# Last stage of a hybrid attention and expert-routed layer on one core: early unscaled residual rows, a ninth weight piece ahead, and single depth steps in the first expert pair

## The chip, the cores and the metric

The kernel runs on one core of a Trainium2 chip. The metric is device time in microseconds (us) of one execution; the kernel before took 2093.07 us (median of three runs, 2092.68 to 2094.48).

## The reference, cut to what matters

One layer for 512 latent tokens of width 2048 (and 256 context tokens, which only give keys and values). All is fp32. Only the second half bears on the change:

```python
x = x + mod_lat[:, 2] * merge_heads(o_m, o_n, g_out_mla[l], g_out_na[l], w_out[l])
h2 = modulate(rms_norm(x, g_norm2[l]), mod_lat[:, 3], mod_lat[:, 4])
x = x + mod_lat[:, 5] * expert_choice_ffn(h2, w_router[l], w_gate[l], w_up[l], w_down[l])

def expert_choice_ffn(h, w_router, w_gate, w_up, w_down):
    aff = softmax(h @ w_router)                  # 16 experts
    g, idx = top_k(aff.T, cap)                   # each expert picks cap = 64 tokens
    xs = h[idx]
    y = (silu(xs @ w_gate) * (xs @ w_up)) @ w_down * g[..., None]
    return zeros.at[idx].add(y)
```

## The kernel before, in words

The first 880 us compute the modulation, the projections and the attention. What follows is staged like this.

**Output projection.** `OUT_PLAN` orders four column blocks of 512, each in two halves of the depth (so eight steps `p`), each over four tiles of 128 tokens. DVE adds every result to the residual `x1` in SBUF (`residual`, L1837 and L1842; semaphore `x1_add`). SyncE (SP) loads the projection's weights, 2 MB a step (`load_w_out`, L605). In the last step, each finished tile is turned (`turn_x1`, L973), multiplied with the router's weights (`route`, L985), its softmax taken on DVE and ACT (`soft`), and the result turned again (`turn_aff`, L1006).

**The choice.** DVE finds each expert's 64 best tokens in eight rounds (L1911, L1913) and marks them (L1915). TensorE turns the marks (L1029) and counts them with a triangular and a ones matrix (L1035); DVE makes the slot numbers (L1921) and from them `member` (L1931), the 0/1 matrix that picks the 128 rows of an expert pair. ACT meanwhile scales `x1` in place by the reciprocal root of each row's mean square (L1408, `x1_scaled`), four tiles.

**The experts.** There are 8 pairs of experts. The weights of one pair are 24 pieces of 2 MB: 16 of gate and up (one for each depth step of 128, `gate_up`, L1115) and 8 of down (`down`, L1145). All 192 pieces are loaded by SP in order (`moe_load`, L657). Eight (`PRE`) go to slots of their own before any is used. After that a piece goes into one of six slots (`RING`), and its load waits until the piece that had the slot is used: the semaphore `moe_used` counts the pieces that TensorE has finished. `SLOT_AT` says where the slots lie; slots 6 and 7 are used once and then hold the accumulators.

```python
for n in range(PRE, PAIRS * PIECES):
    before = n - PRE if n < PRE + RING else n - RING
    sp.wait_ge(moe_used, before + 1)
    moe_load(n)
```

The rows of a pair are picked by products of `x1` with `member`, four depth steps at a time (`gather`, L1064), and taken, scaled and shifted by DVE (`take_xsT`, L1953). In pair 0 these groups stand before the depth steps 0, 2, 6 and 10. Pair 1's rows come another way: the scaled `x1` is stored to HBM as `x1_d` (L673, by SP, behind the eight first pieces and the load of `gate2_b`, L668), `find_rows` (L1072) gives the numbers of the rows, and GpSimd fetches them with an indirect DMA (L1560). `turn_member` (L1088) and `rows_of` (L1081) are two short groups of products at depth steps 12 and 13; the weights that `rows_of` gives are taken by DVE in `take_rows`. After the 16th piece ACT takes the silu (L1424), DVE multiplies (L2008), TensorE turns the result (L1131), and the down pieces follow. `spread` (L1102, L1103) adds the rows back.

The queues that matter here: SP issues every weight load and, before, the stores of `x1_d`; each of its waits holds everything behind it. ACT issues none in this stage, and GpSimd the one gather.

## Time and profile before

| | |
|---|---|
| median of 3 runs | 2093.07 us |
| profiled execution | 2088.43 us |
| its span on the core | 2086.5 us |
| TensorE matmuls busy | 1938.2 us (93%) |
| weight loads of TensorE | 1231.2 us (59%) |
| DVE / ACT / GpSimd busy | 832.6 / 427.1 / 174.4 us |
| moved by DMA | 602.78 MB, mean 289 GB/s |
| mean granted TensorE clock | 0.987 |

The page cuts the span into 40 slices of 52.2 us. Slice 21 (from 1095 us) is where the experts' weights begin. All rows below give times in us from the start of the span.

### The profile page before, as it was taken

Reading aid. Unit: us, or ns where it says so; the run is one execution under the profiler, and the core shown is the slowest. Engines: PE = TensorE matmul, PEld = TensorE weight load, DVE = VectorE, ACT = ScalarE, POOL = GpSimd, SP = SyncE. Lnnn points to the kernel's source line nnn. Section 1 sums busy time; section 2 is a strip of 40 time slices with the busy share of each in tenths; the row PEclk is TensorE's granted clock in tenths of the full one; section 3 lists DMA queues with packets and bytes.
Section 4 is the critical chain, followed back from the end, with each engine's and each line's share of the span. In section 5 each row is a group of like instructions: output and inputs, shape, how many; then the busy total and the mean of one; then the engine's idle time right before and its main releaser. Section 6 shows DMA issues by size and latency. Waiting matters only on the chain.

```text
span 2086.5 us, 25707 instructions
## 1 busy us (share of the span) xinstructions
PE 1938.2 (93%) x10114; PEld 1231.2 (59%) x10114; DVE 832.6 (40%) x1723; ACT 427.1 (20%) x1141; POOL 174.4 (8%) x402
## 2 busy tenths in 40 slices
PE   4899999999999999989996999998989999898988
PEld 2578788878877777768885533433435353443433
DVE  5557877773245555534444131221303021121303
ACT  4223223122145555532222000000000000000000
POOL 0003112011133322200000000000000000000000
PEclk9999999999999999999997999999999999999999
DMA  9937888783122111132228999999999999999998
GB/s 403 421 141 270 325 294 291 270 282 138 46 102 86 45 44 44 43 134 81 81 81 353 395 419 429 427 427 428 427 428 427 428 427 427 428 428 427 426 428 355
DMA packets 77079, 602.78 MB, mean 289 GB/s; under 512 B 7568, under 2 KB 25232, under 8 KB 33568
## 3 DMA queue, kind: packets, MB, share of 16 engines
q1 hardware_dynamic: 64224, 591.11, 70.0%
q10 hardware_dynamic: 12592, 8.98, 1.3%
q8 instruction: 81, 1.33, 0.3%
q0 software_dynamic: 144, 1.05, 0.1%
q14 instruction: 38, 0.31, 0.0%
HBM read 584.32 MB, written 16.79 MB: 288 GB/s over the span
## 4 chain that ended last, share of the span: by engine, by line
PE 50%; DMA 11%; DVE 2%; ACT 2%; issue 1%; POOL 0%; DVEq 0%; ACTq 0%
DMA arena<-in_w_gate_up 10%; PE SM L1115 7%; PE TM L1115 7%; PE SM L1145 6%; PE TM L1145 5%; PE TR L1064 3%; PE MJ L1064 2%; PE TM L919 1%; PE SM L885 1%; PE SN L1102 1%; DMA wor<-in_w_out 1%; PE MJ L817 1%; PE MJ L821 1%; PE SM L890 1%; PE SM L960 1%
## 5 line engine op out<-in xcount | busy, mean ns | idle before, releaser
L1115 PE MATMUL SM<-arena 128*64 128x512 f32 x1024 | 245.0, 598 | 47.2 <-DMA arena<-in_w_gate_up 46.7
L1115 PE MATMUL TM<-arena 128*64 128x512 f32 x1024 | 242.7, 592 | 0.0
L1683 DVE SCALAR_TENSOR_TENSOR arena<-arena,csil 128x512 f32<-128x512 f32 x240 | 180.3, 751 | 46.7 <-DMA arena<-in_w_mod 38.3
L1115 PEld LDWEIGHTS SM<-arena 128*64 128x64 f32 x1024 | 71.0, 136 | 191.4 <-issue 190.5
L1115 PEld LDWEIGHTS TM<-arena 128*64 128x64 f32 x1024 | 78.6, 137 | 141.1 <-issue 141.1
L1145 PE MATMUL SM<-arena 128*64 128x512 f32 x512 | 117.8, 609 | 1.5 <-DVE arena L2011 1.5
L1145 PE MATMUL TM<-arena 128*64 128x512 f32 x512 | 116.9, 599 | 0.0
L1203 ACT ACTIVATE wh<-wr 128x2048 fp32r<-128x2048 f32 (+1 forms) x32 | 58.7, 1835 | 192.4 <-PE TN L720 148.8
L1931 DVE TENSOR_TENSOR arena<-cst,rope_t 128x512 f32<-128x512 f32 x8 | 5.5, 692 | 230.3 <-PE MJ L1088 230.3
L718 PE MATMUL SM<-wh,h_hi 128*128 128x512 f32 (+1 forms) x224 | 89.2, 398 | 7.8 <-DVE h_lo L1631 7.8
L1413 ACT CAST y_hi<-arena 128x512 fp32r<-128x512 f32 x32 | 19.8, 619 | 367.7 <-DVE arena L1967 367.7
L1419 ACT CAST memberT<-MJ 128x512 fp32r<-128x512 f32 x8 | 4.7, 585 | 435.7 <-PE MJ L1088 435.7
L1989 DVE TENSOR_TENSOR arena<-arena,SN 128x512 f32<-128x512 f32 x56 | 38.3, 684 | 123.0 <-PE SN L1103 123.0
L718 PE MATMUL TM<-wh,h_hi 128*128 128x512 f32 (+1 forms) x224 | 87.3, 390 | 0.0
L720 PE MATMUL SM<-wh,h_lo 128*128 128x512 f32 (+1 forms) x224 | 85.9, 384 | 0.0
L719 PE MATMUL SM<-wl,h_hi 128*128 128x512 f32 (+1 forms) x224 | 85.7, 383 | 0.0
L1440 POOL TENSOR_TENSOR st<-st,halves 128x1 f32<-128x1 f32 (+2 forms) x116 | 81.9, 706 | 41.7 <-DVE st L1598 32.1
L720 PE MATMUL TM<-wh,h_lo 128*128 128x512 f32 (+1 forms) x224 | 85.1, 380 | 0.0
L719 PE MATMUL TM<-wl,h_hi 128*128 128x512 f32 (+1 forms) x224 | 85.0, 379 | 0.0
L1609 DVE TENSOR_TENSOR wl<-wr,wh 128x2048 fp32r<-128x2048 f32 (+1 forms) x32 | 70.0, 2186 | 26.8 <-ACT wh L1203 26.7
L1145 PEld LDWEIGHTS SM<-arena 128*64 128x64 f32 x512 | 35.3, 139 | 68.7 <-issue 65.3
L1145 PEld LDWEIGHTS TM<-arena 128*64 128x64 f32 x512 | 33.9, 136 | 66.5 <-issue 66.5
(327 smaller groups left out, 3488.1 us busy)
## 6 DMA issues: line engine op xcount, KB each, us to landing
arena<-in_w_gate_up SPq DMA_DIRECT2D x128, 2048.0 KB, 16.3
arena<-in_w_down SPq DMA_DIRECT2D x64, 2048.0 KB, 25.5
arena<-in_w_mod SPq DMA_DIRECT2D x96, 1024.0 KB, 5.5
wr<-in_w_na SPq DMA_DIRECT2D x24, 1024.0 KB, 7.0
wor<-in_w_out SPq DMA_DIRECT2D x8, 2048.0 KB, 7.9
xT<-in_tokens_t SPq DMA_DIRECT2D x4, 1536.0 KB, 12.6
arena<-in_w_qkv SPq DMA_DIRECT2D x8, 640.0 KB, 5.4
wr<-in_w_qa SPq DMA_DIRECT2D x4, 1024.0 KB, 11.9
```

What stands on the lines that cost most here:

```text
L718: pe.matmul(dst, h_hi[:, k, rows], w_hi[w % 2][:, cols], start=first, stop=False)
L719: pe.matmul(dst, h_hi[:, k, rows], w_lo[w % 3][:, cols], start=False, stop=False)
L720: return pe.matmul(dst, h_lo[:, k, rows], w_hi[w % 2][:, cols], start=False, stop=last)
L817: mm = pe.matmul(MJ[:, 0:QK], cqT[:, k, i * P:(i + 1) * P], wq[g % 2][:, k, :], start=(k == 0), stop=(k == Q_RANK // P - 1))
L1064: mm = pe.matmul(dst[:, i * P:(i + 1) * P], x1[:, tile, k * P:(k + 1) * P], member[:, tile, :], start=(tile == 0), stop=(tile == LT - 1))
L1115: mm = pe.matmul(GU[b][64 * e:64 * e + CAP, :], xsT[:, k, 64 * e:64 * e + CAP], w[:, 2 * (b // 2) + e, (b % 2) * NB:(b % 2 + 1) * NB], sta ...
L1145: mm = pe.matmul(GU[b][64 * e:64 * e + CAP, :], actT[:, f, 64 * e:64 * e + CAP], w[:, 2 * j + e, :], start=(f == 0), stop=(f == KF - 1))
L1203: sc.activation(w_hi[w % 2][:, 0:n], w_raw[w % 3][:, 0:n], ACT.Copy).then_inc(w_high, 1)
L1440: po.tensor_tensor(out_ap, ms, halves[:, 0:n], ALU.pow).then_inc(done, 1)
L1609: ve.tensor_tensor(w_lo[w % 3][:, 0:n], w_raw[w % 3][:, 0:n], w_hi[w % 2][:, 0:n].bitcast(F32), ALU.subtract).then_inc(w_low, 1)
L1683: ve.scalar_tensor_tensor(acc, row, c, acc, ALU.mult, ALU.add).then_inc(mod_step, 1)
L1989: ve.tensor_tensor(dst, dst, src, ALU.add).then_inc(acc_done, 1)
```

## The change

- `x1_d` is stored without scaling and by column blocks: the first three blocks by SP behind the weights of the projection's steps 3, 5 and 7, the last by ACT, tile by tile, after each tile's `route`. ACT's scaling of `x1` in place now waits for all 16 of these stores. The fetched rows of pair 1 are scaled afterwards by ACT; their factors come out of `find_rows` beside the row numbers (`rows_rs`).
- `PRE` is 9: the ninth piece goes to a new slot 8, where `gate1_b`, `gated` and `x1T` were and `gate2_b`, `act` and `actT` will be. It waits for the last residual and the last `route`. `gate2_b` is loaded later, ahead of load number 15, after the tenth piece is used. `member_1` moves to other space.
- Pieces 4 to 7 wait for the last projection result (`y_full`) and no more for DVE's reading of it (`y_free`).
- In pair 0 the rows are picked one depth step at a time (`gather_first`, `take_first`): steps 0 and 1 ahead of piece 0, then step k + 2 behind piece k. `turn_member` and `rows_of` move to behind the depth steps 14 and 15.
- TensorE runs 77 products of constants (`keep_clock`), in six places from the end of the projection to the first pick.

The diff, cut to its core:

```diff
-PRE = 8
+PRE = 9
-SLOT_AT = [4, 5, 0, 2, 6, 7, 1, 3]
+SLOT_AT = [4, 5, 0, 2, 6, 7, 1, 3, 8]
@@ sync
                 load_w_out(p)
+                if p >= 3 and p % 2:
+                    nb = p // 2 - 1
+                    cols = slice(nb * NB, (nb + 1) * NB)
+                    sp.wait_ge(x1_add, LT * (2 * nb + 2))
+                    for tile in range(LT):
+                        sp.dma_start(x1_d[tile * P:(tile + 1) * P, cols], x1[:, tile, cols]).then_inc(x1_out, 16)
             sp.wait_ge(y_full, LT * (2 * MODB - 1))
             for n in range(4):
                 moe_load(n)
-            sp.wait_ge(y_free, LT * 2 * MODB)
-            for n in range(4, PRE):
+            sp.wait_ge(y_full, LT * 2 * MODB)
+            for n in range(4, PRE - 1):
                 moe_load(n)
-            sp.dma_start(gate2_b[:], modrow_d[1:2, :].partition_broadcast(P)).then_inc(gate2_in, 16)
-            for tile in range(LT):
-                sp.wait_ge(x1_scaled, tile + 1)
-                sp.dma_start(x1_d[tile * P:(tile + 1) * P, :], x1[:, tile, :]).then_inc(x1_out, 16)
+            sp.wait_ge(x1_add, LT * 2 * MODB)
+            sp.wait_ge(lg_part, LT * MODB)
+            moe_load(PRE - 1)
             for n in range(PRE, PAIRS * PIECES):
                 before = n - PRE if n < PRE + RING else n - RING
                 sp.wait_ge(moe_used, before + 1)
+                if before == PRE:
+                    sp.dma_start(gate2_b[:], modrow_d[1:2, :].partition_broadcast(P)).then_inc(gate2_in, 16)
                 moe_load(n)
@@ tensor
+            def keep_clock(n):
+                for i in range(n):
+                    pe.matmul(SM[:, 0:P], ident[:], ones[:], start=True, stop=True)
...
                 elif kind == "x1_turn":
+                    if (a, tile) == (MODB - 1, LT - 1):
+                        pe.wait_ge(y_free, LT * 2 * MODB - 1)
+                        keep_clock(7)
                     turn_x1(a, tile)
                 elif kind == "route":
+                    if (a, tile) == (MODB - 1, LT - 1):
+                        keep_clock(2)
                     route(a, tile)
...
+            keep_clock(7)
             turn_aff(LT - 1)
+            keep_clock(56)
...
+            def gather_first(k):
+                if k == 0:
+                    pe.wait_ge(member_set, 1)
+                    pe.wait_ge(x1_scaled, LT)
+                if k >= 2:
+                    pe.wait_ge(xt2_free, k - 1)
+                for tile in range(LT):
+                    mm = pe.matmul((TR, MJ)[k % 2][:, 0:P], x1[:, tile, k * P:(k + 1) * P], member[:, tile, :],
+                                   start=(tile == 0), stop=(tile == LT - 1))
+                mm.then_inc(xt2_full, 1)
...
                 for k in range(KD):
-                    if pair == 0 and k in (0, 2, 6, 10):
-                        gather(0, (k + 2) // 4)
-                        if k == 2:
-                            find_rows()
+                    if pair == 0 and k == 0:
+                        gather_first(0)
+                        gather_first(1)
                     pe.wait_ge(xt2_free, KD * pair + k + 1)
                     gate_up(pair, k)
+                    if pair == 0 and k + 2 < KD:
+                        gather_first(k + 2)
+                    if pair == 0 and k == 2:
+                        find_rows()
...
-                    if k == 12:
+                    if k == (12 if pair else 14):
                         turn_member(pair)
-                    if pair == 0 and k == 13:
+                    if pair == 0 and k == 15:
                         rows_of(0)
@@ scalar
+                if (kind, a) == ("route", MODB - 1):
+                    sc.wait_ge(x1_add, LT * (2 * MODB - 1) + tile + 1)
+                    sc.dma_start(x1_d[tile * P:(tile + 1) * P, D - NB:D], x1[:, tile, D - NB:D]).then_inc(x1_out, 16)
+            sc.wait_ge(x1_out, 16 * LT * MODB)
             for tile in range(LT):
                 sc.wait_ge(e_rsd, 2 * tile + 1)
                 sc.activation(x1[:, tile, :], x1[:, tile, :], ACT.Copy, scale=e_rs[:, tile:tile + 1]).then_inc(x1_scaled, 1)
...
+                if pair == 0:
+                    sc.wait_ge(rows_in, 16)
+                    sc.activation(rows_1, rows_1, ACT.Copy, scale=rows_rs).then_inc(rows_set, 1)
```

DVE's part follows: `members_ahead` first copies the rows' factors into the second column of `token_no`, `take_index` copies them out of PSUM, and `take_first` takes one depth step.

**TensorE, from the last product of the projection to the first pick.** L973/L981 is `turn_x1`, L985/L993 `route`, L1006/L1019 `turn_aff`, L1029/L1049 and L1035/L1056 the choice, L999 of the change `keep_clock`. Before:

```order
L973 MATMUL TR<-cst,arena 128x128 x4
L985 MATMUL MJ<-cst,arena 128x16 x4
L1006 MATMUL SN<-cst,probs_r 16x128
L1006 MATMUL TM<-cst,probs_r 16x128
L1029 MATMUL SN<-cst,arena 128x16 x4
L1035 MATMUL TN<-logits,arena 128x64
```

Of the change:

```order
L999 MATMUL SM<-ones,cst 128x128 x7
L981 MATMUL TR<-cst,arena 128x128 x4
L999 MATMUL SM<-ones,cst 128x128 x2
L993 MATMUL MJ<-cst,arena 128x16 x4
L1019 MATMUL SN<-cst,probs_r 16x128
L999 MATMUL SM<-ones,cst 128x128 x7
L1019 MATMUL TM<-cst,probs_r 16x128
L999 MATMUL SM<-ones,cst 128x128 x56
L1049 MATMUL SN<-cst,arena 128x16 x4
L999 MATMUL SM<-ones,cst 128x128
L1056 MATMUL TN<-logits,arena 128x64
```

The products of the kernel keep their order; constant ones stand between them, 56 where TensorE waits for DVE's eight rounds, and four more behind the choice.

**TensorE, the first depth steps of pair 0.** L1064/L1070 is the pick, L1115/L1146 `gate_up`, L1072/L1103 `find_rows`. Before:

```order
L1064 MATMUL TR<-arena 128x128 x16
L1115 MATMUL SM<-arena 64x512 x4
L1115 MATMUL TM<-arena 64x512 x4
L1115 MATMUL SM<-arena 64x512 x4
L1115 MATMUL TM<-arena 64x512 x4
L1064 MATMUL MJ<-arena 128x128 x16
L1072 MATMUL SN<-cst,arena 128x2 x4
```

Of the change:

```order
L1070 MATMUL TR<-arena 128x128 x4
L1070 MATMUL MJ<-arena 128x128 x4
L1146 MATMUL SM<-arena 64x512 x4
L1146 MATMUL TM<-arena 64x512 x4
L1070 MATMUL TR<-arena 128x128 x4
L1146 MATMUL SM<-arena 64x512 x4
L1146 MATMUL TM<-arena 64x512 x4
L1070 MATMUL MJ<-arena 128x128 x4
```

Eight products stand before the first piece where 16 stood, and four between any two pieces of the first 15.

**SP's queue, around the first pieces.** L657/L659 is `moe_load`, L668/L685 the load of `gate2_b`, L673 the stores of `x1_d`. Before:

```order
L657 DMA arena<-in_w_gate_up 128x4096 [waits y_free]
L657 DMA arena<-in_w_gate_up 128x4096 x3
L668 DMA arena<-modrow_d 128x2048
L673 DMA x_d<-arena 128x2048 [waits x1_scaled] x4
L657 DMA arena<-in_w_gate_up 128x4096 [waits moe_used] x8
```

Of the change:

```order
L659 DMA arena<-in_w_gate_up 128x4096 [waits y_full]
L659 DMA arena<-in_w_gate_up 128x4096 x3
L659 DMA arena<-in_w_gate_up 128x4096 [waits lg_part,x1_add]
L659 DMA arena<-in_w_gate_up 128x4096 [waits moe_used] x6
L685 DMA arena<-modrow_d 128x2048 [waits moe_used]
L659 DMA arena<-in_w_gate_up 128x4096
```

The row stores are gone from here, piece 8 is in their place, and six loads follow it before the seventh, number 15, with `gate2_b` ahead of it.

## Rows read from the trace of the kernel before

**Rows 1.** The page, 40 slices of 52.2 us: what the DMA engines moved.

```profile
GB/s 403 421 141 270 325 294 291 270 282 138 46 102 86 45 44 44 43 134 81 81 81 353 395 419 429 427 427 428 427 428 427 428 427 427 428 428 427 426 428 355
```

**Rows 2.** Windows: stretch, length, busy us and count by engine, PEclk, DMA share, GB/s.

```profile
1300.00:1320.00 20.00, 15.65 (x72) 5.61 (x70) 0.69 (x1) 0.58 (x1) 0.00 (x0) 1.00 1.01 428
...
1660.00:1680.00 20.00, 15.61 (x72) 5.63 (x70) 0.69 (x1) 0.58 (x1) 0.00 (x0) 1.00 1.00 425
```

**Rows 3.** Chain of waits in the last pair: start, us, what.

```profile
2007.23 24.82 DMA arena<-in_w_gate_up
```

**Rows 4.** Timeline of SP's queue: start, us, engine, line, DMA.

```profile
1094.53 29.29 SPq L657 DMA_DIRECT2D arena<-in_w_gate_up  x8
1123.86 0.50 SPq L668 DMA_DIRECT2D arena<-modrow_d  x1
1128.97 6.00 SPq L673 DMA_DIRECT2D x_d<-arena  x4
...
1154.37 0.33 SPq L657 DMA_DIRECT2D arena<-in_w_gate_up  x1
...
1190.46 0.33 SPq L657 DMA_DIRECT2D arena<-in_w_gate_up  x1
...
1201.25 0.33 SPq L657 DMA_DIRECT2D arena<-in_w_down  x1
...
1228.01 0.33 SPq L657 DMA_DIRECT2D arena<-in_w_down  x1
```

**Rows 5.** L657's landings: the load issued at 1190.46, then that at 1220.30.

```profile
DMA to landing us min/median/max: 7.7/7.7/7.7
...
DMA to landing us min/median/max: 14.4/14.4/14.4
```

**Rows 6.** Chain of waits from the choice to the first down piece.

```profile
1141.89 1.90 PE TN L1035 x8
...
1157.76 3.77 PE MJ L1064 x32
1161.53 0.79 PE SN L1072 x8
1162.32 1.87 PE SM L1115 x8
...
1188.71 1.72 PE TM L1115 x8
...
1212.25 1.00 PE TR L1081 x8
...
1220.94 1.30 DVE arena L2008 x2
...
1224.32 3.65 PE SM L1145 x16
```

**Rows 7.** TensorE's timeline, 1120 to 1151: start, us, line, operation, idle time before.

```profile
1123.94 1.75 PE L985 MATMUL MJ<-cst,arena 128*128 128x16 f32 x8 [0.68 <-ACT arena L1384]
...
1140.97 0.60 PE L1029 MATMUL SN<-cst,arena 16*128 16x16 f32 x4 [13.01 <-DVE arena L1915]
...
1144.82 5.35 PE L1064 MATMUL TR<-arena 128*128 128x128 f32 x32 [1.04 <-DVE arena L1931]
```

**Rows 8.** Windows, as in group 2: the stretch in which the clock fell.

```profile
1124.00:1128.00 4.00, 2.28 (x10) 1.68 (x10) 1.56 (x9) 1.85 (x5) 0.93 (x3) 0.52 0.90 385
```

**Rows 9.** Timelines of DVE, GpSimd and ACT around the choice.

```profile
1144.08 0.69 DVE L1931 TENSOR_TENSOR arena<-cst,rope_t 128x512 f32<-128x512 f32 x1
...
1125.06 0.55 POOL L1440 TENSOR_TENSOR st<-st,halves 128x1 f32<-128x1 f32 x1
...
1126.96 7.67 ACT L1408 ACTIVATE arena<-arena,st 128x2048 f32<-128x2048 f32 x4
```

**Rows 10.** DMA issues, KB each and us to landing: one at 574.77, then the page's.

```profile
v_d<-arena ACTq DMA_DIRECT2D x1, 256.0 KB, 9.0
...
x_d<-arena SPq DMA_DIRECT2D x4, 1024.0 KB, 22.9
```

More of the change, by code:

```diff
@@ L369, in build_layer @@
         member = arena.take(192 * K, LT, P)
-        member_1 = arena.take(136 * K, LT, P)
+        member_1 = arena.take(152 * K, LT, P)
         rows_1 = arena.take(152 * K, D)
@@ L415, in build_layer @@
         idx_1 = st[:, 24:25].bitcast(U32)
+        rows_rs = st[:, 25:26]
         x_ms, x_rstd = st[:, 0:AT], st[:, 6:6 + AT]
@@ L500, in build_layer @@
             sem(n) for n in ("silu_done", "act_done", "at2_full", "at2_free", "y_done"))
-        idx_full, idx_set, x1_out, rows_in = sem("idx_full"), sem("idx_set"), sem("x1_out"), sem("rows_in")
+        idx_full, idx_set, x1_out, rows_in, rows_set = (
+            sem(n) for n in ("idx_full", "idx_set", "x1_out", "rows_in", "rows_set"))
         y_high, y_low, mt_full, mt_set, add_full, acc_done = (
@@ L1030, in _ @@
             mm.then_inc(pick_full, 1)
+            keep_clock(1)
             pe.wait_ge(pick_set, 2)
@@ L1037, in _ @@
             mm.then_inc(pick_full, 1)
+            keep_clock(4)
+            def gather_first(k):
[8 more added lines that the diff above has]
+                mm.then_inc(xt2_full, 1)
             def gather(pair, q):
                 if q == 0:
-                    pe.wait_ge(member_set, pair + 1 + (pair > 0))
-                    if pair:
-                        pe.wait_ge(pay_set, 2 * pair)
-                    else:
-                        pe.wait_ge(x1_scaled, LT)
-                if q == 1 and pair:
+                    pe.wait_ge(member_set, pair + 2)
+                    pe.wait_ge(pay_set, 2 * pair)
+                if q == 1:
                     pe.wait_ge(mt_set, pair)
-                if 4 * pair + q >= 2:
-                    pe.wait_ge(xt2_free, 16 * pair + 4 * (q - 1))
+                pe.wait_ge(xt2_free, 16 * pair + max(4 * (q - 1), 0))
                 dst = (TR, MJ)[q % 2]
@@ L1054, in gather @@
                     if q == 0:
-                        pe.wait_ge(rows_in, 16)
+                        pe.wait_ge(rows_set, 1)
                     for i in range(4):
@@ L1070, in find_rows @@
                 pe.wait_ge(member_set, 2)
+                pe.wait_ge(idx_set, 1)
                 for tile in range(LT):
@@ L1123, in turn_act @@
                 if pair == 0:
-                    pe.wait_ge(idx_set, 1)
+                    pe.wait_ge(idx_set, 2)
                 for q in range(2):
@@ L1555, in _ @@
                 po.tensor_tensor(e_inv[:, one], e_ms[:, one], e_rs[:, one], ALU.mult).then_inc(e_rsd, 1)
-            po.wait_ge(idx_set, 1)
-            po.wait_ge(x1_out, 16 * LT)
+            po.wait_ge(idx_set, 2)
+            po.wait_ge(x1_out, 16 * LT * MODB)
             po.indirect_dma_start(rows_1, None, x1_d, bass.IndirectOffsetOnAxis(ap=idx_1, axis=0)).then_inc(rows_in, 16)
@@ L1936, in members_ahead @@
             def members_ahead():
+                ve.wait_ge(e_rsd, 2 * LT)
+                ve.tensor_copy(token_no[:, :, 1], e_rs).then_inc(idx_set, 1)
                 ve.tensor_tensor(member_1.rearrange("p t (e s) -> p t e s", s=CAP),
@@ L1945, in take_index, with take_first @@
                 ve.wait_ge(idx_full, 1)
+                ve.tensor_copy(rows_rs, SN[:, 1:2])
                 ve.tensor_copy(idx_1, SN[:, 0:1]).then_inc(idx_set, 1)
+            def take_first(k):
+                ve.wait_ge(xt2_full, k + 1)
+                ve.tensor_scalar(xsT[:, k, :], (TR, MJ)[k % 2][:, 0:P], mul2[:, k:k + 1], shift2[:, k:k + 1],
+                                 ALU.mult, ALU.add).then_inc(xt2_free, 1)
             def take_xsT(pair, q):
-                ve.wait_ge(xt2_full, 4 * pair + q + 1)
+                ve.wait_ge(xt2_full, KD + 4 * (pair - 1) + q + 1)
                 src = (TR, MJ)[q % 2]
@@ L1991, in _ @@
             members(0)
-            take_xsT(0, 0)
+            take_first(0)
+            take_first(1)
             members_ahead()
-            take_xsT(0, 1)
+            for k in range(2, 5):
+                take_first(k)
             take_index()
-            take_xsT(0, 2)
-            take_xsT(0, 3)
+            for k in range(5, KD):
+                take_first(k)
             take_rows(0)
```

## The prediction

> **What bounds the kernel now.** Read the page's slices first [rows 1]. From slice 24 on the DMA engines move 426 to 429 GB/s in every slice but the last, while TensorE has idle time in each pair: 15.65 and 15.61 us busy out of 20 in two windows where the DMA runs at 428 and 425 [rows 2]. So the stream of expert weights sets the pace. At 428 GB/s a piece of 2.097 MB takes 4.90 us; TensorE needs 1.87 + 1.72 = 3.59 us for one in the gate and up half [rows 6]. In the last pair the chain of waits goes through a 24.82 us wait on such a load [rows 3], so the end of the kernel follows the arrival of the last gate and up piece. The question is therefore only this: **from what moment is the stream never interrupted again, and how many bytes are still ahead of it then?** What TensorE gains elsewhere in this stage is worth nothing by itself.
>
> SP's queue answers it for the kernel before [rows 4]. I number the pieces from 0. Pieces 0 to 7 are issued in the stretch from 1094.53 to 1123.86, then come `gate2_b` (1 MB) and the four row stores (4 MB), and piece 8 is issued at 1154.37, when piece 0 is used. Pieces 9 to 13 follow quickly, but number 14 must wait until piece 8 is used: TensorE ends it at 1188.71 + 1.72 = 1190.43 and SP issues at 1190.46 [rows 4, 6]. That load lands after only 7.7 us [rows 5], so it found the queue empty: the stream had stopped. Number 16, issued at 1201.25 when piece 10 is used, also comes just too late. From there nothing stops: number 21, issued at 1220.30, lands 14.4 us later [rows 5], at 1234.7, with others in front of it. Eight pieces (14 to 21) thus take 1234.7 - 1190.46 = 44.2 us, of which 8 x 4.90 = 39.2 is transfer and 5.0 is latency, start-up and the second stop. I give that second stop 1.0 us, an estimate between zero and the 3.7 us that 5.0 leaves if a lone landing costs 7.7 - 4.9 = 2.8 us, rather low, since number 21 has a landing lag of its own.
>
> **The change, part by part.**
>
> *Clock and choice.* The granted clock fell to half while TensorE waited for DVE: 0.52 in 1124 to 1128 [rows 8]. Constant products fill these waits. I take it that the clock holds. Then L985, 1.75 us for 8 records [rows 7], ends about 0.9 earlier, but the softmax waits for GpSimd's root too, which ends at 1125.06 + 0.55 = 1125.61 [rows 9], so I take 0.35 us of it. `turn_aff` gives 0.1, L1029 (0.60 us) 0.25 and L1035 (1.90 us) halves to 0.95 [rows 6, 7]: 1.6 us in all. `member` was ready at 1144.08 + 0.69 = 1144.77 [rows 9], and will be at about 1143.2. The filler of 56 must not outlast the choice: the pick's products ran 32 records in 3.77 us at full clock [rows 6], two records a product, so 56 take 56 x 0.236 = 13.2 us as the upper bound; TensorE's wait is 13.01 us long [rows 7], and the eight rounds are as long as before. It fits or costs 0.2 us.
>
> *First pick by depth steps.* Before, 16 products stood ahead of piece 0, 5.35 us, partly at half clock [rows 7]; now 8, half of 3.77, with a small start 2.0 us. Piece 0 ends at 1143.2 + 2.0 + 3.65 = 1148.9, and not 1154.37. DVE's take of step 0 hides behind the pick of step 1. But from here on every piece carries its own pick. A quarter of 3.77 is 0.94; a group of 8 small records behind another kind took 0.79 and 1.00 [rows 6], so the bounds are 0.94 and 1.15. I take 1.02, nearest the quarter, since the products are the same. And a piece behind a pick costs 3.59 instead of 3.44 (its first half is 1.87 and not 1.72 us). A step is 3.59 + 1.02 = 4.61 us.
>
> *Ninth piece.* It puts 4.90 us of weights into time in which the DMA is idle or stored rows. But six loads follow it (9 to 14), and **number 15 must wait until piece 9 is used**. That is 1148.9 + 9 x 4.61 + 0.79 (L1072) = 1191.2. By then number 14, issued when piece 5 is used (near 1173), has long landed: the stream stands still from about 1183 to 1192, where before it stood for 1 us. The prefetch is nearly all given back here.
>
> *Rows and `gate2_b`.* The row stores (4 MB, 9.8 us of DMA) leave a place where nothing waited for them but the stream's own start, and go where the slices show 81 GB/s [rows 1]: no cost. SP's new waits on `x1_add` end about 1.5 us after the projection's result, some 20 us ahead of the next weight load: none. `gate2_b` stands right ahead of number 15, 1.05 MB or 2.45 us, in full on the path. ACT's scaling of the fetched rows (7.67 / 4 = 1.9 us [rows 9]) lies 40 us ahead of its use. `rows_of` behind piece 15 (1.00 us [rows 6]) puts `take_rows` and `members` ahead of DVE's L2008, by my estimate 1.5 us; so the down pieces start near 1224.0 (piece 15 ends near 1218.4) and not at 1224.32 [rows 6]. The first is used by 1227.6, as in SP's row at 1228.01 [rows 4]; number 22 can be issued then, 1 to 2 us before the stream runs dry. This hides, narrowly.
>
> *The sum.* From the gate to the landing of number 21: before 44.2 us for eight pieces. After: one piece less (-4.9), `gate2_b` (+2.45), no second stop (-1.0) = 40.75 us. 1191.2 + 40.75 = 1231.95 against 1234.7: **2.7 us earlier**, and everything behind it is the same stream. With 0.1 off for the filler: 2.6. The profiled execution would take 2088.43 - 2.6 = 2085.8 us. The median of the runs stands 4.64 us above that execution; I carry the difference over: 2090.5 us. Bounds: the pick at 0.94 gives 0.7 more, at 1.15 1.2 less; the second stop at 0 or 3.7 gives -1.0 or +2.7.
>
> **The rivals.** (0.2%, 4.2 us, is about what a measurement of this kernel can tell from no change.)
>
> 1. *Small steps cost nothing* (chance 0.22). If products and weight loads of pick and piece interleave so that a step takes 3.44 + 0.89, piece 9 ends at 1188.7 and the gain is 5.2 us: 2087.9. The second stop's upper bound lands in the same place. For it: TensorE starts many records before the last has ended. Against it: 1.87 against 1.72 behind each switch [rows 6].
>
> 2. *The last row store is late: slower* (0.11). ACT scales `x1` only when all stores have landed, and the pick needs all four tiles. ACT issues the last one near 1124.9, 3 us behind four pieces of 2 MB on SP's queue. Scaling takes 7.67 us [rows 9], so it must land by 1143.2 - 7.67 = 1135.5. The stores of before took 22.9 us [rows 10], in SP's queue; if this one also waited for the pieces it would land near 1145, and `member` would wait 9.4 us: gate at 1200.6, 6.7 us slower than before, 2099.8. Against it: a store of the same size from ACT's queue, beside loads of 0.5 to 2 MB on SP's, landed in 9.0 us [rows 10]; here that is 1133.9, 1.6 us to spare. It decides beyond 10.6 us; at 13.3 us beyond the issue the whole gain is gone.
>
> 3. *Whole turns of the DMA engines* (0.05). If an engine takes a long run of SP's rows before it turns to ACT's store, one or two pieces go first: 4.9 to 9.8 us, with 2.8 us of latency the store lands by 1137.5, 2.0 us late, and the gain shrinks to 0.6: 2092.5. The row of 9.0 us does not exclude it. The Trainium skill ("DMA: Bandwidth & Descriptors", "Queues, rings and completion order") says that each DMA engine turns from queue to queue, but drains a whole packet of one, some 9 to 17 descriptors, before it does. By that rule this rival is the case to expect; the trace has no store beside a full stream of pieces.
>
> 4. *The clock falls in spite of the filler* (0.06). Then products of the 56 run at half rate and TensorE is still busy with them when the choice is made. All of them at half rate take 13.2 us more, and the gate comes 13 to 14 us later: 2104. But the pick of before, products of the same form, took 5.35 us where 3.77 is full rate [rows 6, 7], so the clock came back within it. A quarter of the 13.2 us, 3.3, gives 2093.8, which I take. For it: before, the clock fell around the short waits just ahead of the choice [rows 7, 8], and the filler there is only 7 and 2 products.
>
> 5. The forecast itself has 0.56: the gate at piece 9, gain between 1 and 4 us.
>
> **How the numbers follow.** Faster by over 0.2% is rival 1, and a little of the forecast's upper bound: 0.26. Slower is rival 2: 0.11. The rest is 0.63 (of rival 4 I leave the worst end out). The range goes from 2086.5 (rival 1 with 1.4 us from the last pair, whose clock may fall or not) to 2096.0, which takes in rivals 3 and 4 and a store that is late by half of rival 2's.
>
> **What would show it.** In SP's queue: piece 8 near 1125, number 9 near 1149, `gate2_b` and number 15 together near 1191, no store of rows there. In windows: the DMA below a tenth from about 1184 to 1191; clock 1.0 from 1124 to 1148. `gather_first` about 1 us each; DVE's `member` at 1143. ACT's four scalings end ahead of it. The forecast is wrong if the DMA does not stop before number 15, if number 22 lands with the queue empty, or if TensorE's first pick waits for ACT.

## The result and the profile after

| | before | changed |
|---|---|---|
| median of 20 runs each, same chip | 2092.57 us | 2096.36 us |
| lowest to highest | 2089.20 to 2095.93 | 2089.41 to 2101.96 |
| profiled execution | 2088.43 us | 2097.87 us |
| its span | 2086.5 us | 2096.1 us |
| mean granted clock | 0.987 | 0.991 |

The ratio is 1.0020, 95% interval 1.0014 to 1.0026: **slower by 3.8 us**, just outside the forecast range (2096.0). The forecast was 2090.5 and 2.6 us faster.

The page of the changed kernel, its line of busy times and the slices that answer to [rows 1]:

```profile
PE 1960.2 (94%) x10268; PEld 1251.3 (60%) x10268; DVE 834.5 (40%) x1725; ACT 429.3 (20%) x1142; POOL 172.2 (8%) x402
...
GB/s 402 407 145 274 322 297 291 273 282 141 37 100 84 46 44 44 48 129 101 101 101 345 314 410 429 428 428 427 427 428 427 427 428 428 427 428 428 426 428 355
```

In slices 18 to 20 stand 101 and no more 81 GB/s: the stored rows. From slice 24 on no slice differs by more than 1 GB/s. So the loss lies ahead of it, and I cut the profiled time there into three stretches at two of SP's issues: the load for the projection's step 2 and the first expert piece. SP's queue before, then after:

```profile
943.97 124.38 SPq L605 DMA_DIRECT2D wor<-in_w_out  x6
```

```profile
946.69 25.51 SPq L607 DMA_DIRECT2D wor<-in_w_out  x2
973.39 1.91 SPq L669 DMA_DIRECT2D x_d<-arena  x4
...
1104.20 79.04 SPq L659 DMA_DIRECT2D arena<-in_w_gate_up  x15
...
1201.61 0.33 SPq L685 DMA_DIRECT2D arena<-modrow_d  x1
1201.97 0.43 SPq L659 DMA_DIRECT2D arena<-in_w_gate_up  x1
```

| stretch | before | after | difference |
|---|---|---|---|
| start to 944 / 946.69 | 943.97 | 946.69 | +2.7, ahead of anything changed |
| to the first expert piece (projection) | 150.56 | 157.51 | **+6.95** |
| first expert piece to the end | 991.97 | 991.90 | **-0.07** |

I take the 2.7 us as scatter between executions: the profiled one of before is 4.1 us under its median, that of the change 1.5 us above, and in the traces of the twelve runs below this first stretch takes anything from 944.4 to 949.8 us. What counts is that the projection, where I forecast nothing, lost 7 us in this execution, and that the expert stage, where I forecast 2.6 us, gained nothing. These are two failures, with two causes.

**The projection.** The chain of waits goes, in every second step, through the landing of the weights (each row: start, us, what). Before, then after:

```profile
969.15 7.72 DMA wor<-in_w_out
1018.55 7.81 DMA wor<-in_w_out
1068.02 8.49 DMA wor<-in_w_out
```

```profile
971.88 9.08 DMA wor<-in_w_out
1022.64 9.09 DMA wor<-in_w_out
1073.38 9.58 DMA wor<-in_w_out
```

These are the loads that have row stores behind them (steps 3, 5, 7). Each lands 1.1 to 1.4 us later, 3.7 us in all, and ACT's and DVE's splitting of the weights and the products wait for it. The rest, 3.2 us, is the clock (the last section has the sum for every trace). Windows of the two kernels (columns as in [rows 2]), before and then after:

```profile
1080.00:1090.00 10.00, 9.11 (x44) 7.41 (x44) 4.63 (x8) 1.53 (x4) 0.00 (x0) 1.00 0.00 0
1090.00:1100.00 10.00, 10.00 (x45) 8.26 (x44) 2.04 (x4) 0.00 (x0) 0.00 (x0) 1.00 0.45 157
```

```profile
1080.00:1090.00 10.00, 8.01 (x44) 6.74 (x42) 7.33 (x9) 4.99 (x7) 0.00 (x0) 0.96 0.36 134
1090.00:1100.00 10.00, 10.00 (x34) 8.13 (x35) 1.55 (x4) 0.00 (x0) 0.00 (x0) 0.70 0.00 0
```

TensorE now waits 2.0 us of these ten, where it waited 0.9; behind it the granted clock falls to the lower of its two levels, 1.2 GHz, for 6.8 us, from 1089.2 to 1096.0 (0.96 and 0.70 over the two windows, 34 records in the second in place of 45), which it did not do here before.

**The expert stage.** Up to load 21 it went nearly as forecast. ACT scaled in time, the filler ended in time, the DMA stood still where I said. ACT's timeline; TensorE's; then windows:

```profile
1143.20 7.68 ACT L1446 ACTIVATE arena<-arena,st 128x2048 f32<-128x2048 f32 x4 [6.78 <-DMA x_d<-arena]
```

```profile
1137.06 12.67 PE L999 MATMUL SM<-ones,cst 128*128 128x128 f32 x112
1150.24 0.42 PE L1049 MATMUL SN<-cst,arena 16*128 16x16 f32 x4 [0.52 <-DVE arena L1956]
```

```profile
1192.00:1196.00 4.00, 4.00 (x24) 2.02 (x24) 0.41 (x1) 0.00 (x0) 0.00 (x0) 1.00 0.34 143
1196.00:1200.00 4.00, 4.00 (x24) 1.75 (x22) 0.41 (x1) 0.00 (x0) 0.00 (x0) 1.00 0.00 0
1200.00:1204.00 4.00, 4.00 (x24) 1.82 (x22) 0.41 (x1) 0.00 (x0) 0.00 (x0) 1.00 0.29 92
...
1232.00:1236.00 4.00, 3.43 (x14) 2.72 (x16) 2.63 (x6) 0.00 (x0) 0.00 (x0) 0.57 0.99 416
...
1240.00:1244.00 4.00, 4.00 (x21) 1.41 (x21) 2.54 (x8) 0.00 (x0) 0.00 (x0) 1.00 0.94 315
1244.00:1248.00 4.00, 4.00 (x19) 1.53 (x16) 1.44 (x2) 0.62 (x1) 0.00 (x0) 1.00 0.97 360
```

The last two windows are the surprise: a second dip of the stream, 315 and 360 GB/s, where the kernel before moved 428. I follow loads 21, 22 and 23 through SP's issues and their landings. After:

```profile
1229.14 0.33 SPq L659 DMA_DIRECT2D arena<-in_w_down  x1
DMA to landing us min/median/max: 12.9/12.9/12.9
...
1239.32 0.33 SPq L659 DMA_DIRECT2D arena<-in_w_down  x1
DMA to landing us min/median/max: 8.6/8.6/8.6
...
1243.92 0.33 SPq L659 DMA_DIRECT2D arena<-in_w_down  x1
DMA to landing us min/median/max: 10.1/10.1/10.1
```

Before, loads 22 (issued at 1228.01, [rows 4]) and 23 took 11.6 and 11.8 us; 21 is in [rows 5]:

```profile
DMA to landing us min/median/max: 11.6/11.6/11.6
...
1232.62 0.33 SPq L657 DMA_DIRECT2D arena<-in_w_down  x1
DMA to landing us min/median/max: 11.8/11.8/11.8
```

Issue plus landing, counted from the issue of the first expert piece (1094.53 and 1104.20), here and in all that follows. The *gate* is the first load whose slot is held by a piece that was itself loaded on demand, number 14 before and 15 after the change:

| | before | after | gain |
|---|---|---|---|
| gate load issued (14 / 15) | +95.9 | +97.8 | |
| load 21 landed | +140.2 | +137.8 | 2.3 |
| load 22 issued | +133.5 | +135.1 | |
| load 22 landed | +145.1 | +143.7 | 1.4 |
| load 23 landed | +149.9 | +149.8 | 0.1 |
| load 24 landed | +154.8 | +154.7 | 0.1 |
| last gate and up load landed | +937.5 | +938.4 | -0.9 |

The gain of 2.3 us was there at load 21 and was gone two loads later. The 0.9 us at the last load are not the change's: behind load 24 the stream has stops of its own, whose sum differs from trace to trace by as much (see "Behind load 24" at the end). The last row's load, in the changed kernel's chain of waits:

```profile
2017.09 25.55 DMA arena<-in_w_gate_up
```

Load 22 was issued only 2.7 us ahead of the landing of load 21 (before: 6.7 us), and 22 and 23 landed 5.9 and 6.1 us behind their forerunners in place of 4.9.

### The profile page after: what moved, and what is told of

It reads as the page before. It is cut to its first block, busy times and chain, and to the rows that moved or that the text cites. A ratio compares the mean times of both kernels' runs of the same rounds, so it can differ in the third digit from the quotient of the medians.

```text
span 2096.1 us, 26033 instructions
## 1 busy us (share of the span) xinstructions
PE 1960.2 (94%) x10268; PEld 1251.3 (60%) x10268; DVE 834.5 (40%) x1725; ACT 429.3 (20%) x1142; POOL 172.2 (8%) x402
## 4 chain that ended last, share of the span: by engine, by line
PE 50%; DMA 12%; DVE 2%; ACT 2%; issue 1%; POOL 0%; DVEq 0%; ACTq 0%
DMA arena<-in_w_gate_up 9%; PE SM L1146 8%; PE TM L1146 7%; PE SM L1176 5%; PE TM L1176 5%; PE TR L1094 2%; PE MJ L1094 2%; PE TM L927 1%; PE SM L893 1%; DMA wor<-in_w_out 1%; DMA arena<-in_w_down 1%; PE SN L1133 1%; PE MJ L825 1%; PE MJ L829 1%; PE SM L968 1%
## 5 line engine op out<-in xcount | busy, mean ns | idle before, releaser
L1146 PE MATMUL SM<-arena 128*64 128x512 f32 x1024 | 245.6, 599 | 45.8 <-DMA arena<-in_w_gate_up 45.7
L1146 PE MATMUL TM<-arena 128*64 128x512 f32 x1024 | 242.8, 592 | 0.0
L1146 PEld LDWEIGHTS SM<-arena 128*64 128x64 f32 x1024 | 70.2, 136 | 185.6 <-issue 183.8
L1146 PEld LDWEIGHTS TM<-arena 128*64 128x64 f32 x1024 | 78.7, 137 | 141.0 <-issue 141.0
```

Source lines behind the costliest of these rows:

```text
L1146: mm = pe.matmul(GU[b][64 * e:64 * e + CAP, :], xsT[:, k, 64 * e:64 * e + CAP], w[:, 2 * (b // 2) + e, (b % 2) * NB:(b % 2 + 1) * NB], sta ...
```

## The experiments

Twelve kernels, in four groups, each group beside runs of the kernel before on its own chip (medians 2090.77, 2091.73, 2091.35, 2091.75 us). All are edits of the changed kernel but the second. "Last landing" is the row of the chain as in [rows 3], counted from the first expert piece (before: +937.5, changed: +938.4). From load 24 to there the fourteen traces take 782.7 to 784.3 us, so last landings less than 1.6 us apart decide nothing, and where two kernels are close I give the landing of load 24 too (before +154.8, changed +154.7). Each kernel has one trace; each ratio rests on all its executions.

**1. The row stores wait until the weights ahead of them have landed.**

```diff
                     sp.wait_ge(x1_add, LT * (2 * nb + 2))
+                    sp.wait_ge(wo_in[p % 2], 16 * (p // 2 + 1))
                     for tile in range(LT):
```

> The changed kernel, with one more wait: SP issues the four row stores behind the weights of steps 3, 5 and 7 only when these weights have landed. Theory S (the row stores share the DMA engines with the projection's weights, which land in 9.1, 9.1 and 9.6 us after the issue and not in 7.7, 7.8 and 8.5, and this delays the projection): the landings are back at 7.7 to 8.5, the stage from the load of step 2 to the first piece takes 150 to 151.5 us and not 157.5, the kernel is 3.5 to 4 us faster than the changed one and within 1 us of the kernel before. Rival T (the stage is longer by the clock, which fell to half for 6.8 us in it, or by chance): the landings may be shorter, but the time stays 3 to 4 us above the kernel before.

Measured 2091.27 us, ratio 1.0002 (0.9993 to 1.0011). The three landings are back, and the clock holds; chain, window and SP's queue:

```profile
972.34 7.88 DMA wor<-in_w_out
1021.88 8.06 DMA wor<-in_w_out
1071.57 8.58 DMA wor<-in_w_out
```

```profile
1080.00:1090.00 10.00, 9.02 (x44) 7.34 (x43) 6.15 (x8) 5.00 (x7) 0.00 (x0) 1.00 0.31 105
1090.00:1100.00 10.00, 10.00 (x45) 8.29 (x45) 2.88 (x4) 0.00 (x0) 0.00 (x0) 1.00 0.13 26
```

```profile
947.15 25.51 SPq L607 DMA_DIRECT2D wor<-in_w_out  x2
...
1098.19 79.05 SPq L659 DMA_DIRECT2D arena<-in_w_gate_up  x15
```

The projection takes 151.0 us, 6.5 less than with the change. One wait of SP takes away the whole loss. The traces of all the other kernels agree: the four whose stores go out at once (changed, runs 2, 3 and 4) take 155.4 to 158.4 us for the projection, the nine with this wait 150.6 to 152.7. The expert stage is as before it (load 22 at +135.2, last landing +937.9).

**2. The kernel before with the early, unscaled row stores alone** (and what they need: fetched rows scaled afterwards).

```diff
                 load_w_out(p)
+                if p >= 3 and p % 2:
+                    sp.wait_ge(x1_add, LT * (2 * nb + 2))
+                    for tile in range(LT):
+                        sp.dma_start(x1_d[...], x1[...]).then_inc(x1_out, 16)
```

> The kernel before, with the early unscaled row stores alone (blocks 0 to 2 by SP behind the weights, block 3 by ACT, rows scaled after the fetch): no ninth piece, picks by four, no filler. Theory S: slower than the kernel before by 3.5 to 4.5 us, all of it ahead of the first piece. The gate of load 14 stays at about 96 us behind the first piece's issue, since TensorE sets it. Rival T: no difference in the projection, time within 1 us of the kernel before.

Measured 2096.08 us, ratio 1.0022 (1.0013 to 1.0032). This one part makes a loss as large as the whole change. The chain of waits:

```profile
971.74 8.72 DMA wor<-in_w_out
1022.13 9.33 DMA wor<-in_w_out
1076.36 8.92 DMA wor<-in_w_out
```

The projection takes 158.4 us (before: 150.6), with 0.83 of the clock in 1030 to 1050; from the first piece to the end it is 992.2 us (before: 992.0).

**3. `gate2_b` is loaded after piece 8, in the gap, and not beside load 15.**

```diff
+                if before == PRE:
+                    sp.wait_ge(moe_used, PRE)
+                    sp.dma_start(gate2_b[:], ...).then_inc(gate2_in, 16)
                 sp.wait_ge(moe_used, before + 1)
-                if before == PRE:
-                    sp.dma_start(gate2_b[:], ...).then_inc(gate2_in, 16)
```

> The changed kernel, but gate2_b is loaded when piece 8 is used, one piece ahead of load 15, and so in the stretch in which the DMA stands still. Theory G (number 15 waits until piece 9 is used, and gate2_b's 2.45 us stand in the stream behind it): gate2_b costs nothing, number 15 lands 2.4 us earlier against its gate; whether it reaches the end depends on the stop ahead of number 22, which in the changed kernel was already there: 0 to 2.4 us faster than the changed kernel, more likely under 1, because number 22 waits for the first down piece. Rival: a full 2.4 us faster, if the stop at number 22 came only from the clock in that one profile.

Measured 2094.94 us, ratio 1.0020 (1.0009 to 1.0030). Load 15 lands 2.1 us earlier, load 21 only 0.9 (+136.9), load 22 0.2 us earlier (+143.5): `gate2_b`'s bytes had mostly covered stops of the stream that come anyway. Load 24 lands 0.9 us earlier (+153.7); the last landing is +936.8, the rest of its 1.7 us being within the scatter behind load 24. As a mend it is small, and the ratio is that of the changed kernel.

**4. No filler** (`keep_clock` returns at once).

> The changed kernel without the 77 constant products. Theory: the clock falls to half as before, member is ready 1.6 us later against the last projection product, the first two picks run partly at half rate, so piece 0 ends 2.5 to 3 us later and the gate of load 15 too: the kernel is 2 to 3 us slower than the changed one. Rival (the stop ahead of number 22 is what decides, and the filler's effect ends there as well, or the filler itself costs something): within 1 us of the changed kernel.

Measured 2098.87 us, ratio 1.0036 (1.0023 to 1.0048), on six executions; that is 3.3 us more than the changed kernel's 1.0020, and the two intervals just overlap. The clock is at the lower level through the choice and the first pick, which takes twice as long. Window, and TensorE's timeline (with the filler the two picks took 1.16 and 1.06 us):

```profile
1140.00:1148.00 8.00, 0.61 (x4) 0.50 (x4) 6.99 (x15) 7.01 (x4) 0.00 (x0) 0.50 1.00 428
...
1151.04 2.08 PE L1069 MATMUL TR<-arena 128*128 128x128 f32 x8 [1.04 <-DVE arena L1971]
1152.91 1.91 PE L1069 MATMUL MJ<-arena 128*128 128x128 f32 x8
```

Gate +101.4 (with filler +97.8), load 24 +157.2 (+154.7), last landing +940.9: the filler is worth 2.5 us of the expert stage to this kernel. It is the one part of the change that a run shows to pay.

**5. As 1, and `rows_of` behind piece 14 and not 15.**

```diff
-                    if pair == 0 and k == 15:
+                    if pair == 0 and k == 14:
                         rows_of(0)
```

> Kernel e1 (the changed kernel with the row stores behind the landed weights), and rows_of stands behind depth step 14 and not behind 15, so that DVE takes the weights and builds the next member ahead of the silu. Theory D (the stop ahead of load 22 is the end of the new order: rows_of and its takers hold DVE's product by 1.4 us, and this longer wait lets TensorE's clock fall): from piece 15's end to the first down piece's use takes 7.7 us as before the change and not 10.2, load 22 is issued about 134 us after the first piece and not 135.2, and the kernel is 1 to 2 us faster than e1. Rival: same as e1, since the gate of load 15 alone sets the stream.

Measured 2090.81 us, ratio 0.9994 (0.9986 to 1.0003). Load 22 is issued at +133.5 and not +135.2, load 24 lands at +153.5 (run 1: +154.3), the last landing is +936.7. In the changed kernel DVE takes the weights and makes the next `member` between the last piece and `L2059`, which TensorE waits for:

```profile
1230.13 0.34 DVE L2010 COPY st<-TR 64x1 f32<-64x1 f32 x2 [8.34 <-PE TR L1112]
1230.50 0.69 DVE L1972 TENSOR_TENSOR arena<-cst,rope_t 128x512 f32<-128x512 f32 x1
1231.22 1.29 DVE L2059 TENSOR_TENSOR arena<-TM,arena 128x512 f32<-128x512 f32 x2
```

So the delay of `rows_of` did not hide. It has a second effect: behind this wait the clock falls for 3.4 us (changed: 1232.5 to 1236.0) in the traces of the changed kernel and of runs 1, 3, 6, 7 and 10, all with `rows_of` behind piece 15, and in none of the five that have it behind piece 14 (5, 8, 9, 11, 12); run 4, without the filler, has `rows_of` late and kept its clock here. This run is also the test of how early load 22 is issued: gate and load 21 are where run 1 has them (issue +97.8; landing +137.9 and +137.8), load 22 is issued 1.7 us earlier, and load 24 lands 0.8 us earlier.

**6. As 1, with eight pieces ahead as before** (`PRE = 8`, `gate2_b` right behind piece 7).

> Kernel e1 with the ninth piece undone: eight pieces ahead, gate2_b behind them as before the change. Theory N (the ninth piece only moves the gate from piece 8 to piece 9): load 14 is issued when piece 8 is used, 4.67 us ahead of where e1 issues load 15, and gate2_b is out of the way: the kernel is as fast as e1 or up to 2 us faster. Rival P (a piece fetched ahead is 4.9 us less to load later): 2.4 to 4.9 us slower than e1.

Measured 2093.64 us, ratio 1.0005 (0.9996 to 1.0014). Load 24 lands at +154.1 (run 1: +154.3), the last at +938.4 (+937.9). With `gate2_b` moved along, the ninth piece is worth nothing that the trace shows at load 24: what it moves ahead is lost in the longer standstill before the gate, as forecast.

**7. As 1, with the rows of pair 0 picked four depth steps at a time** (ahead of steps 0, 2, 6, 10, as before).

```diff
-                    if pair == 0 and k == 0:
-                        gather_first(0)
-                        gather_first(1)
+                    if pair == 0 and k in (0, 2, 6, 10):
+                        gather_first((k + 2) // 4)
```

> Kernel e1 with the picks of pair 0 by four depth steps again (ahead of steps 0, 2, 6 and 10). Theory M (load 15 waits for piece 9, and until then TensorE must do the picks of 12 steps in 3 groups instead of 11 steps in 11 groups): piece 0 is used 1.8 us later than in e1, but piece 9 1 to 1.5 us earlier, and the kernel is 0.5 to 1.5 us faster than e1. Rival F (the first piece's use starts the stream and decides): 1.8 us slower than e1.

Measured 2089.96 us, ratio 0.9994 (0.9985 to 1.0004). TensorE starts piece 0 2.3 us later than in run 1 (+53.2 and +50.9), but has the gate at +96.8 (+97.8), ends piece 15 3.2 us earlier, and load 22 is issued at +131.9 (+135.2). The step from 21 to 22 is 4.9 us: no dip. Load 24 lands at +151.8, 2.6 us earlier than in run 1, and the last landing is +934.9, 3.0 us earlier. The chain there has one pick of four steps in 3.77 us, where four single ones cost 4 x 1.09 and four switches of 1.87 - 1.72 = 0.15 us: 4.96. **With the single depth steps undone, the trace has the tail that the change was forecast to give.** The median does not settle it: the interval takes in no change.

**8. As 5, with `gate2_b` in the gap.**

> The changed kernel with three mends: row stores behind the landed weights, gate2_b in the gap, rows_of behind step 14. Theory: the 2.45 us of gate2_b and the 1 to 2 us of rows_of only pay together, since each alone is caught by the other stop: 2.5 to 3.5 us faster than e1, and so 2 to 3 us faster than the kernel before the change. Rival: no more than e5 gives.

Measured 2091.06 us, ratio 0.9997 (0.9989 to 1.0006). Load 22 is issued at +133.5 in both this and run 5. Load 24 lands at +153.0 against +153.5 there, the last at +937.0 against +936.7: `gate2_b`'s move buys 0.6 us up to load 24, which the scatter behind it hides, and the median shows nothing. The 2.5 to 3.5 us that I expected over run 1 are not there.

**9 and 10. Picks by four, `gate2_b` in the gap; 9 also with `rows_of` behind piece 14.**

> The changed kernel with four mends: row stores wait for the weights' landing, picks by four depth steps, gate2_b in the gap (after piece 8), rows_of one step earlier. Measured from the issue of the first expert piece: gate of load 15 at +96.5 to +97, load 22 near +130.2 (picks by four alone had +131.85, rows_of earlier alone gained 1.7). Theory L (the tail is set by whichever comes later, the landing of load 21 or the issue of load 22): both come earlier here, so the landing of the last pair's last gate and up load comes at +931 to +933.5, against +934.9 with picks by four alone and +937.5 before; total 2088 to 2089 where before is 2091.7, ratio 0.998 to 0.9988. Rival (gate2_b and rows_of buy nothing more, as gate2_b bought nothing when added to the earlier rows_of): +934.9, total as with picks by four alone, ratio 0.9994.

> As the run with four mends, but rows_of stays behind piece 15. Load 22 near +131.9 as with picks by four alone. Theory L: gate2_b's 2.45 us leave the stream's path, but load 22 is then issued less than 3 us before the queue runs dry, so only part is gained: the last gate and up load lands at +933 to +934.5. Rival (gate2_b buys nothing): +934.9. If the gate2_b load were worth its full 2.45 us: +932.4.

Measured 2087.70 us, ratio **0.9984 (0.9976 to 0.9993)**, and 2087.55 us, ratio 0.9986 (0.9977 to 0.9995): both faster than the kernel before, by 3.7 and 3.8 us. But load 24 lands at +151.8 and +151.9 where run 7 had +151.8, and the last landings are +934.7 and +934.8 where it had +934.9: the rival held, my theory on these two edits did not. The chains of 7, 9 and 10, each a row of its own view:

```profile
2011.48 25.15 DMA arena<-in_w_gate_up
```

```profile
2006.84 24.95 DMA arena<-in_w_gate_up
```

```profile
2005.41 24.79 DMA arena<-in_w_gate_up
```

(First expert pieces at 1101.75, 1097.14 and 1095.39.) Why: a pick of four follows piece 9, so load 16 comes 7.35 us behind load 15, and without `gate2_b` the DMA waits there. A window of run 9:

```profile
1200.00:1204.00 4.00, 4.00 (x22) 1.31 (x20) 0.00 (x0) 0.00 (x0) 0.00 (x0) 1.00 0.58 152
```

Load 16 lands at +112.6 in runs 7 and 9 alike. That the medians of 9 and 10 stand lower against before than that of 7 is within the intervals, which overlap.

**11 and 12. Picks of 2, 4, 4 and six single steps; 12 with `gate2_b` back beside load 15.**

```diff
+STARTS = [0, 2, 6, 10, 11, 12, 13, 14, 15, 16]
+PICK_AT = [0, 1, 5, 9, 10, 11, 12, 13, 14]
```

> Row stores behind the landing, gate2_b after piece 8, rows_of behind piece 14, and the depth steps of pair 0 picked in groups of 2, 4, 4 and then six single ones, so that 11 steps and not 12 are picked by the end of piece 9 and no group of four follows the gate. Times from the issue of the first expert piece. Theory C (gate2_b bought nothing in the run with four mends because its 2.45 us had covered the wait for load 16, which came 7.35 us behind load 15 there): here load 16 follows 4.7 us behind load 15, so the gap is not filled by it and both gains count. Gate of load 15 at +95.5, load 22 at +129 to +131, no dip of the DMA between 1196 and 1240; last gate and up load lands at +931.4 to +932.5 (four mends: +934.65). Total 2 to 3 us below the run with four mends: ratio to before 0.997 to 0.998. Rival D (the tail is bound by the issue of load 22 or by something later, and neither gate2_b nor the gate matter): +934 to +935, ratio 0.9984.

> The run before with gate2_b put back beside load 15, where the change has it; nothing else differs. Theory C: with single steps behind the gate there is no wait of the stream for gate2_b to cover, so its 2.45 us are now in full on the path: last gate and up load lands 2 to 2.5 us later than in the run before, at +933.5 to +935. Rival D: no difference (within 0.4 us).

Measured 2088.62 us, ratio 0.9985 (0.9974 to 0.9997), and 2089.30 us, ratio 0.9991 (0.9981 to 1.0000). Last landing +935.5 and +935.6, as the rival had it. But at load 24 run 11 is 0.9 us ahead (+151.3 and +152.2): there `gate2_b` in the gap is worth something, though 0.9 and not the 2 to 2.5 us of my theory. Behind load 24 run 11 takes 784.2 us and run 12 783.3, within the scatter of all the traces, and so the 0.9 us are gone at the end. Gate and load 22 came later than I had worked out (+96.3 and +132.3).

## Why the prediction was wrong, point by point

**"No cost" for the row stores failed**, in the part *Rows and `gate2_b`*. I read a mean of 81 GB/s over 52 us [rows 1] as room. But the loads of the projection come in bursts, 2 MB in 7.7 us, with the chain of waits on their landing; each store was issued 1.5 us behind one of them. The price was 1.1 to 1.4 us a load and, with the clock, 6.9 us of the profiled projection. In the trace's packet records the last 16 KB row of these loads ends 8.8, 8.8 and 9.2 us behind the issue (before: 7.4, 7.5 and 7.9), and the first 2 KB rows of the stores start at 7.3 to 7.5, ahead of it. By medians it is 5.3 us for the stores alone (run 2), and run 1 takes it away with one wait. I had asked when SP's next wait ends, not what the DMA was doing. None of my rivals had this place: rival 2 looked at the last store only. The Trainium skill ("DMA: Bandwidth & Descriptors", "Two DMAs through the same engine are not ordered") says that descriptors of one queue start in order but are pipelined; by the order of starting alone the stores behind a load would cost it nothing, and the landings of runs 1 and 2 show that here they do.

**"This hides, narrowly" failed.** The gate's forecast was +96.7 and it came at +97.8, half of it since a step was 4.67 us and not 4.61 (the pick 1.09 and not 1.02). The sum had load 21 at +137.4, and it was +137.8: good to 0.4 us, but with luck, since three of its terms were off. The second stop of before was not 1.0 us: of the 5.0 us a lone landing of 2.8 leaves 2.2 (and not 3.7, as the prediction has it for its upper bound), and the landings show them, loads 16 and 17 following 6.5 and 5.6 us behind their forerunners in place of 4.9. The changed kernel has a stop there too, 6.3 us at load 17, where the sum had none. And `gate2_b` cost 1.8 us and not 2.45: load 15 lands 9.4 us behind its issue, in run 3 without it 7.6. But load 22 had to keep pace. I had it at +133.1; it came at +135.1, 1.0 us by the steps, the rest by `rows_of` on DVE and by the clock at 1232 to 1236 (0.57). And even on time it would have been late: I called 1 to 2 us before the end of the transfers enough, though I had myself put a lone landing 2.8 us above its transfer. Runs 5, 7, 9 and 10 move load 22 forward and the tail follows: +936.7, +934.9, +934.7, +934.8 (load 24: +153.5, +151.8, +151.8, +151.9). So the step that failed is that load 22 keeps pace: of the forecast gain of 2.6 us, 2.3 were there at load 21 and 0.1 at load 23.

**Where it was right.** The filler (0.52 us of idle time left behind it; run 4). `member` at +48.8, forecast +48.7. The standstill of the DMA before load 15, and that it takes back the ninth piece (run 6). `gate2_b` on the path of load 15. Behind load 22 little of it is left: at load 24 its move is worth 0.6 to 0.9 us where single steps follow the gate (run 8 against 5, 3 against the changed kernel, 11 against 12) and nothing where a pick of four does (10 against 7).

**Rivals.** 1: the step has 1.09 us for the pick, not 0.89: no. 2: the last row store, issued by ACT at 1133.01, took 10.2 us, just under the limit of 10.6; ACT ended scaling at 1150.9, `member` was set at 1153.0: no, but it was near. 3: not as told, but it was near. Pieces 4 to 7 were issued 0.6 to 2.6 us ahead of that store on SP's queue (the first four had landed by 1128.95), and it landed at 1143.18, behind piece 4 (1138.28) and just ahead of piece 5 (1143.61); the store issued at 1126.01, with little left in SP's queue, took 3.6 us. In the packet records its 128 rows of 2 KB start between 1136.6 and 1142.6, and 114 of them start as one of SP's 16 KB rows ends. So the engines did not take long runs of SP's rows: they took turns row by row, which on 16 engines is 8 turns of 0.61 us, 4.9 us in all. The Trainium skill's rule ("DMA: Bandwidth & Descriptors", "Queues, rings and completion order"), that an engine drains a packet of one queue, some 9 to 17 descriptors, before it turns, is not what this trace shows. 4: clock 1.0 from 1124 to 1232: no.

**What is shown and what is argued.** That the stores cost the projection its time is shown from both sides (runs 1 and 2). That single depth steps cost the tail is shown by the trace of run 7 against that of run 1. That it goes through the issue of load 22 is shown from both sides: run 5 moves it with the gate and load 21 in place and gains 0.8 us at load 24, and run 9 issues it 1.4 us earlier than run 10, where the lead is long enough already, and gains 0.1. Why a stop comes with leads that look long enough is open.

## What to carry to other kernels

- A mean rate is no room for a transfer. Ask which load on the critical chain is under way when the store is issued, and issue it behind that load's landing; one wait did it.
- When a stream is to be kept full, list all loads that are issued on demand up to the steady state. Here the gain passed the first such load and was lost at the eighth, because the work between the pieces had grown (14 small picks in place of 3 large ones) and `rows_of` had moved behind the last of them.
- A first piece that starts 2.3 us earlier is worth nothing if the steps behind it are longer: count the total up to the point that the stream waits for.

## What the runs showed that was not expected

**How early a load must be issued.** The lead is the time from a load's issue to the landing of the load before it; the step is the time between the two landings.

| load 22 (and 23) | lead, us | step, us |
|---|---|---|
| before | 6.7 | 4.9 |
| run 9 | 6.9 | 4.9 |
| run 10 | 5.6 | 4.9 |
| run 7 | 5.3 | 4.9 |
| run 2 (22; 23) | 6.3; 6.6 | 4.9; 5.3 |
| run 5 (22; 23) | 4.5; 5.7 | 5.8; 4.9 |
| run 12 (22; 23) | 4.4; 5.6 | 5.8; 4.9 |
| run 4 (22; 23) | 3.7; 5.1 | 6.0; 4.9 |
| run 8 (22; 23) | 3.1; 4.1 | 5.6; 5.9 |
| changed (22; 23) | 2.7; 4.0 | 5.9; 6.1 |
| run 1 (22; 23) | 2.6; 3.7 | 5.7; 6.0 |
| run 6 (22; 23) | 2.3; 3.9 | 6.2; 5.5 |
| run 3 (22; 23) | 2.2; 4.1 | 6.5; 5.4 |
| run 11 (22; 23) | 3.7; 4.0 | 4.9; 5.5 |

With 5.1 us or more all but one of these landed 4.9 us behind their forerunners; with 4.5 or less, all but one came 0.5 to 1.6 us late. The lead alone does not decide everywhere: load 17 had 5.1 to 5.3 us in the changed kernel and in runs 1, 5, 6 and 12 and took 6.1 to 6.4, while in runs 4 and 7 it had 5.1 and 5.4 and took 4.9. For loads 22 and 23, a queue that is full to the last microsecond was already too empty: about one whole piece had to lie ahead.

**Behind load 24.** From there to load 183, the last of the gate and up half, the queue is never short (5.6 us of lead or more), and still every trace has 3 to 12 steps of 5.1 to 6.5 us in place of 4.9. Most come in series about 207 us apart: in the kernel before at loads 61, 103 and 145, landing at +337.4, +544.5 and +751.5, 6.4 us each. They are in the kernel before as in all the others, so no edit here makes them; what does is open. A landing far down the stream is therefore a poor measure of what an edit did at its start.

**Late landings and the clock add up.** For each trace: how much later than before the loads of steps 3, 5 and 7 land, in sum; half of the time for which the projection had the lower clock (an estimate: work at half rate); and how much longer the projection took.

| | landings, us | half of the time at the lower level, us | sum, us | projection, us |
|---|---|---|---|---|
| changed | 3.7 | 3.4 | 7.1 | 6.9 |
| run 2 | 2.9 | 5.1 | 8.0 | 7.8 |
| run 3 | 4.4 | 1.7 | 6.1 | 6.0 |
| run 4 | 3.3 | 1.7 | 5.0 | 4.9 |
| run 11 | 0.6 | 1.7 | 2.3 | 2.1 |
| runs 1, 5 to 10, 12 | 0.1 to 1.4 | 0 | 0.1 to 1.4 | 0.0 to 1.4 |

**The clock and TensorE's waits.** In steps 3, 5 and 7 TensorE waits once for the weights, up to 1.4 us before and in the nine kernels with run 1's wait, 1.1 to 2.1 us in the four without. The granted clock fell to the lower level behind five of those twelve waits, for 3.4 or 6.8 us, and behind one of the other thirty (run 11, behind 1.0 us). The length of the wait alone does not decide: the changed kernel lost its clock behind 2.0 us, but run 3 kept it behind 2.1:

```profile
1090.00:1100.00 10.00, 7.88 (x40) 6.63 (x39) 4.62 (x8) 1.25 (x4) 0.00 (x0) 1.00 0.00 0
1100.00:1110.00 10.00, 10.00 (x46) 8.29 (x45) 2.04 (x4) 0.00 (x0) 0.00 (x0) 1.00 0.48 174
```
